# An RWKV chunk scan on 64x64 quadrants of TensorE: half of the products moved to the two quadrants left idle

## What is computed

```python
def step(S, inp):
    r_t, w_t, k_t, v_t, kk_t, b_t = inp
    sa = jnp.einsum('bhij,bhj->bhi', S, -kk_t)
    S = (S * w_t[:, :, None, :] + sa[..., None] * b_t[:, :, None, :]
         + v_t[..., None] * k_t[:, :, None, :])
    return S, jnp.einsum('bhij,bhj->bhi', S, r_t)
```

## Time and profile before

| what | value |
|---|---|
| median of 3 runs | 3131.69 us |
| the profiled execution, its own time | 3130.24 us |
| its span, first to last instruction | 3128.4 us |
| mean granted TensorE clock, share of full | 0.970 |
| busy, PE (matmul) / DVE / ACT / POOL | 93% / 57% / 34% / 41% |
| RWKV scan, loads issued to last DVE copy | 2288.0 to 2510.3 us |

### The profile page before, as it was taken

One profiled execution on the slowest core, in us unless ns is written; L12 is line 12 of the kernel. 1 busy time (PEld: TensorE's weight loads), 2 busy tenths in 40 slices (PEclk: granted clock), 3 DMA queues, 4 the chain that ended last, 5 costly groups with the idle time before them and its releaser, 6 DMA issues. The chain is left out here.

```text
span 3128.4 us, 48977 instructions
## 1 busy us (share of the span) xinstructions
PE 2918.8 (93%) x18460; PEld 2411.1 (77%) x18460; DVE 1784.2 (57%) x2599; ACT 1064.8 (34%) x1666; POOL 1283.0 (41%) x649
## 2 busy tenths in 40 slices
PE   7899889999999999999999999979869967999997
PEld 5677678887888888878888888856769855788775
DVE  1354359965777777057777777763846654333115
ACT  3366233343333333321121211244423444433223
POOL 3522333554444444444444444433344322344442
PEclk9999999999999999999999999989989998999998
DMA  3211222454444644655555555522662101222231
GB/s 120 78 58 55 75 94 78 141 147 131 165 165 164 215 169 169 208 186 197 198 189 187 193 199 195 177 80 76 206 168 54 31 14 54 71 97 94 101 101 68
DMA packets 173745, 404.23 MB, mean 129 GB/s; under 512 B 55344, under 2 KB 55472, under 8 KB 172336
## 3 DMA queue, kind: packets, MB, share of 16 engines
q1 hardware_dynamic: 173616, 402.39, 39.2%
HBM read 318.45 MB, written 83.89 MB: 129 GB/s over the span
## 5 line engine op out<-in xcount | busy, mean ns | idle before, releaser
L158 POOL TENSOR_TENSOR weights_low<-weights_raw,weights_high 128x1024 fp32r<-128x1024 f32 x435 | 1129.2, 2596 | 1597.9 <-ACT weights_high L150 1597.9
L150 ACT ACTIVATE weights_high<-weights_raw 128x1024 fp32r<-128x1024 f32 x435 | 460.7, 1059 | 1638.5 <-PE psum L258 1621.4
L256 PE MATMUL psum<-expert_in_high,weights_high 128*128 128x512 f32 x1152 | 458.3, 398 | 9.0 <-DVE expert_in_low L351 4.5
L257 PE MATMUL psum<-expert_in_low,weights_high 128*128 128x512 f32 x1152 | 449.7, 390 | 0.0
L258 PE MATMUL psum<-expert_in_high,weights_low 128*128 128x512 f32 x1152 | 449.5, 390 | 0.0
L256 PE MATMUL psum<-coefficients_high,weights_high 128*128 128x512 f32 x1024 | 399.6, 390 | 5.9 <-DVE coefficients_low L1211 4.2
L257 PE MATMUL psum<-coefficients_low,weights_high 128*128 128x512 f32 x1024 | 399.3, 390 | 0.0
L258 PE MATMUL psum<-coefficients_high,weights_low 128*128 128x512 f32 x1024 | 399.2, 390 | 0.0
L1211 DVE TENSOR_TENSOR coefficients_low<-activation_in,coefficients_high 128x512 fp32r<-128x512 f32 x128 | 354.9, 2772 | 4.4
L256 PEld LDWEIGHTS psum<-expert_in_high,weights_high 128*128 128x128 f32 x1152 | 217.1, 188 | 57.0 <-issue 9.8
L258 PEld LDWEIGHTS psum<-expert_in_high,weights_low 128*128 128x128 f32 x1152 | 216.9, 188 | 45.4
(11 more groups left out here) (381 smaller groups left out, 4647.5 us busy)
## 6 DMA issues: line engine op xcount, KB each, us to landing
weights_raw<-in_weights SPq DMA_DIRECT2D x437, 512.0 KB, 3.4
expert_activations<-expert_activation SPq DMA_DIRECT2D x128, 256.0 KB, 4.0
coefficient_table<-table_stage SPq DMA_DIRECT2D x8, 4096.0 KB, 13.1
table_group<-coefficient_table SPq DMA_DIRECT2D x128, 256.0 KB, 4.1
activation_in<-expert_activations SPq DMA_DIRECT2D x128, 256.0 KB, 3.7
chunk_b_k_v<-scan_vectors SPq DMA_DIRECT2D x8, 768.0 KB, 5.7
scan_vectors<-scan_stage SPq DMA_DIRECT2D x4, 1280.0 KB, 6.6
scan_vectors<-scan_stage SPq DMA_DIRECT2D x4, 1024.0 KB, 6.1
```

Of the source, the lines that this page charges most:

```text
L150: act.activation(d.hi[:, m % SPLIT, :], d.raw[:, m % RAW, :], ACT.Copy).then_inc(d.high, 1)
L158: pool.tensor_tensor(d.lo[:, m % SPLIT, :], d.raw[:, m % RAW, :], d.hi[:, m % SPLIT, :].bitcast(F32), ALU.subtract).then_inc(d.split, 1)
L256: pe.matmul(acc, w[0][:, cols], x[0], start=start, stop=False)
L257: pe.matmul(acc, w[0][:, cols], x[1], start=False, stop=False)
```

## The change

`product` becomes a generator with two new arguments, `side` (which half the operands lie in) and `out` (which half the result goes to). HEAD is the half in which a head's inputs lie, TOKEN the other. The scores and the turns go from HEAD to TOKEN, y goes from TOKEN to HEAD: these use the quadrants (rows 0-63, columns 64-127) and (rows 64-127, columns 0-63). Everything else stays in TOKEN, on the two quadrants that were in use. `beside` merges two products matmul pair by matmul pair.

```diff
-                def product(bank, key, g, width, terms, at=0, last=True):
+                def product(bank, key, g, width, side, out, terms, at=0, last=True):
...
-                            for r in HALVES:
-                                mm = pe.matmul(bank.ps[r, cols], lhs(r, g * H + u), rhs(r, g * H + u),
+                            for r in range(2):
+                                row = HALVES[r ^ side]
+                                mm = pe.matmul(bank.ps[HALVES[r ^ out], cols], lhs(row, g * H + u), rhs(row, g * H + u),
                                                start=(j == 0), stop=(j == len(terms) - 1))
-                    if last:
-                        mm.then_inc(bank.made, 1)
+                            if last and u == H - 1 and j == len(terms) - 1:
+                                mm.then_inc(bank.made, 1)
+                            yield
...
+                def beside(first, second, ratio=1):
+
+                    for n, _ in enumerate(first):
+                        if n % ratio == ratio - 1:
+                            next(second, None)
+                    alone(second)
...
+                    for g in range(2):
+                        if tail:
+                            alone(solve(i - 1, g))
+                        alone(grow(i, 1, g))
+                    for g in range(2):
+                        if tail:
+                            beside(itertools.chain(state(i - 1, g), times_x(i, 2, g)), y(i - 1, g))
...
+                        beside(both(grow, i, 2), scores(i + 1, 0, 0), 2)
+                        beside(both(times_x, i, 3), scores(i + 1, 0, 1), 2)
+                        beside(both(grow, i, 3), scores(i + 1, 1, 0), 2)
+                        beside(both(times_x, i, 4), scores(i + 1, 1, 1), 2)
+                        beside(both(grow, i, 4), bk_t(i + 1, 0))
+                        beside(both(times_x, i, 5), bk_t(i + 1, 1))
+                        beside(grow(i, 5, 0), v_t(i + 1, 0))
+                        beside(grow(i, 5, 1), v_t(i + 1, 1))
```

`rhs` and y leave out the term with the state for chunk 0 (it is zero), and the state after the last chunk is no longer computed. `state_out` now also waits for y of its group, since y reads the old state:

```diff
+                    if i == 0:
+                        dve.wait_ge(ends_in, 32)
+                        dve.tensor_tensor(S[:, half(g), :], view(hb[g], C), decay, ALU.mult).then_inc(hb[g].read, 1)
+                        return
+                    hb[g].taken(dve, ("S", g, i - 1))
+                    tb[g].full(dve, ("y", i))
...
-                for g in range(2):
-                    state_out(NCH - 1, g)
```

The inputs a and r are needed in both halves. They are loaded twice: with b (`front_in`), k and v (`back_in`) into two buffers `vec`, and a second time with the halves swapped (`load_ar`, two DMAs a chunk). The chunk decays are copied with swapped halves once. To make room, ar and L lie in the residual h, which is stored to DRAM in `mixer_inputs` and read back beside `gla_scan`:

```diff
                 for s in range(SLOTS):
                     w.load(sp, 0, s, SLOTS)
+                    if s == 3:
+                        sp.wait_ge(final_scaled, DC)
+                        sp.dma_start(dram["residual"], h[:, :, :]).then_inc(h_out, 16)
...
+                load_vec(0)
+                load_vec(1)
+                gla.sync(sp)
+                for r in range(2):
+                    sp.dma_start(turned_ends[HALVES[1 - r], :, :], ends[HALVES[r], :, :]).then_inc(ends_in, 16)
                 load_ar(1)
...
+                sp.dma_start(k.h[:, :, :], dram["residual"]).then_inc(h_in, 16)
+                sp.wait_ge(h_in, 16)
```

More of the change, by code:

```diff
@@ L10 @@
+import itertools
 from contextlib import ExitStack
@@ L2184, in _ @@
-                    if tail:
-                        state(i - 1, 0)
-                    times_x(i, 2, 1)
-                    if tail:
-                        y(i - 1, 1)
-                    grow(i, 2, 0)
-                    if tail:
-                        state(i - 1, 1)
-                    grow(i, 2, 1)
-                    if head:
-                        scores(i + 1, 0, 0)
-                    times_x(i, 3, 0)
-                    if head:
-                        scores(i + 1, 0, 1)
@@ L2212, in _ @@
-                    grow(i, 4, 1)
-                    if head:
-                        v_t(i + 1, 0)
-                    times_x(i, 5, 0)
-                    if head:
-                        v_t(i + 1, 1)
-                    times_x(i, 5, 1)
-                    grow(i, 5, 0)
-                    grow(i, 5, 1)
+                        alone(rhs(i - 1, 0))
+                        alone(rhs(i - 1, 1))
+                    alone(both(times_x, i, 1))
+                    for g in range(2):
+                        if tail:
+                            alone(solve(i - 1, g))
+                        alone(grow(i, 1, g))
@@ new lines, in _ @@
+                    for g in range(2):
+                        if tail:
+                            beside(itertools.chain(state(i - 1, g), times_x(i, 2, g)), y(i - 1, g))
+                        else:
+                            alone(times_x(i, 2, g))
+                    if head:
+                        beside(both(grow, i, 2), scores(i + 1, 0, 0), 2)
[6 more added lines that the diff above has]
+                        beside(grow(i, 5, 1), v_t(i + 1, 1))
+                    else:
+                        alone(both(grow, i, 2))
+                        for l in range(3, LV):
+                            alone(both(times_x, i, l))
+                            alone(both(grow, i, l))
@@ L2221, in _ @@
                 for g in range(2):
-                    rhs(NCH - 1, g)
+                    alone(rhs(NCH - 1, g))
                 for g in range(2):
-                    solve(NCH - 1, g)
+                    alone(solve(NCH - 1, g))
                 for g in range(2):
-                    y(NCH - 1, g)
-                    state(NCH - 1, g)
+                    alone(y(NCH - 1, g))
             @block.scalar
@@ L2268, in _ @@
                     gla.scalar(act, i, 1)
-                    if tail:
-                        y_out(i - 1, 0)
-                    w_out(i, 2, 0)
-                    w_out(i, 2, 1)
-                    if tail:
-                        y_out(i - 1, 1)
+                    for g in range(2):
+                        w_out(i, 2, g)
+                        if tail:
+                            y_out(i - 1, g)
                     gla.scalar(act, i, 2)
@@ L2365, in _ @@
                         k_masks(i + 1, 0)
-                    grown(i, 3, 0)
+                    for g in range(2):
+                        grown(i, 3, g)
                     if head:
                         b_masks(i + 1, 1)
-                    grown(i, 3, 1)
-                    if head:
                         k_masks(i + 1, 1)
```

162 lines of the change are left out of this document (72 added, 90 removed).

## The result

| | before | after |
|---|---|---|
| median of 7 runs each, us | 3131.27 | 3140.42 (3136.31 to 3143.03) |
| ratio, 95% interval | | 1.0029 (1.0018 to 1.0040) |
| profiled execution, its span, us | 3130.24, 3128.4 | 3140.42, 3138.4 |
| seven chunk steps, us | 175.63 | 184.47 |
| last copy of y on ACT | 2507.11 | 2515.78 |

The change is 9 us slower, a little over what a measurement can tell, and the profile agrees: the span grew by 10.0 us, the seven steps by 8.8. From the issue of the scan's first load to the last copy of y pass 226.5 us (from 2289.24) against 219.2 (from 2287.96): 7.4 of the 10.0 us lie in the scan, 1.3 ahead of it and 1.3 behind.

What follows compares the result with a forecast made beforehand. TensorE's own list of work was taken to bound the scan. Savings of 18.2 (seven steps) + 2.0 + 1.9 + 0.9 + 1.0, less 1.0, made 23 us, hence 3109 us; range 3088 to 3136.

Steps and rivals of the forecast that it cites:

- Do four quadrants run at once?: TensorE in the scan: a third and fourth quadrant likely run at once with the two in use, moving 9.1 us a step.
- The chain as the new bound: Chunk steps: with 14.0 us left on TensorE, the chain through ACT and DVE shows; 23.77 us become 20.8 to 21.4.
- The walk: Level-by-level timing of a light chunk step like 4, from its first `times_x` to the next chunk's, at 20.8 to 21.4 us.
- Rival B: TensorE in the scan: issue-bound at 29 ns a record, so four quadrants get no more; 3128 us, chance 0.12.
- Rival C: TensorE in the scan: quadrants on shared rows serialize and the order loses cover, 2.1 us a step; 3143 us, chance 0.16.
- the last state: End of the scan: 32 matmuls of 1.87 us and a DVE pair are left out, 1.9 us saved.
- the zero term: The zero state's term in rhs: 16 matmuls are left out, 0.9 us saved; in y it is hidden.
- the start: Start of the scan: the first scores wait for 768 KB instead of 1280 KB; 1.0 us saved.
- the store: The 2 MB residual store behind the mixer's fourth weight load holds the DMA engines: 1 us lost, bounds 0 and 3.
- Chunk 7: Last chunk, level 1 to level 3: 9.35 us become 7.3, 2.0 us saved.
- The second load: Second load of a and r, 0.5 MB a chunk, needed a chunk step after issue: costs nothing.
- The signs named: Changed profile: 16 `grow` matmuls beside one scores product in 0.9 to 1.0 us if right, 1.4 (B), 1.8 (C); steps 21 to 23.

Runs made afterwards that it cites:

- e3: The changed kernel with its own order but on the two quadrants of the kernel before: 3149.11 us, ratio 1.0050 to the kernel before.
- e2: The changed kernel with the order and two quadrants of the kernel before, so only storage, loads and other small parts remain: 3130.72 us, ratio 1.0000.
- e8: The kernel before plus a 512 KB DRAM to DRAM copy behind the loads of chunks 2 to 7, nobody waiting for it: 3133.44 us, ratio 1.0007.
- e10: The changed kernel with levels 4 and 5 in the order of the kernel before on TensorE and ACT: 3138.34 us, ratio 1.0021 to the kernel before.
- e11: The changed kernel with levels 1 to 3 in the order of the kernel before on all engines: 3139.49 us, ratio 1.0021 to the kernel before.
- e16: The kernel before with turns on VectorE from a swapped copy, b scores in level 3, k scores in level 4, GLA inputs loaded earlier: 3117.59 us, ratio 0.9956.
- e1b: The changed kernel plus a TensorE-only block of eight matmul series behind the scan; 512 matmuls on four quadrants: 29.1 us written out, 17.9 in a loop.

## Why the prediction was wrong

It said 3109, range 3088 to 3136, with 0.71 for faster; it is 3140, on the side that had 0.16.

- **Do four quadrants run at once?** Right, as the earlier trace rows suggested: 58 ns for four records, 17.9 us in the loop against 29.9 for two quadrants. The Trainium skill ("TensorE: Matmul & The Clock Gate", "The mechanism" of array packing) lets a weight load overlap a running matmul only when the row groups differ; read as the prediction reads it, four quadrants would have taken the 29.9 of two in the loop. The trace disagrees, and the measurement decides.
- **The chain as the new bound, 20.8 to 21.4 us a step.** This step failed. The walk let TensorE go through 14.0 us of work at 58 ns a matmul wherever its operands were ready. The steps took 23.4 to 28.9 us. For level 2 it had 2 x 1.4 us for state, `times_x` and y; they took 6.76 (2441.62 to 2448.38), with two block gaps in them (1.61 and 1.80). The sum lacked the supply of instructions: 4 for an fp32 matmul, 256 a block, 3.8 us a block; the 5.75 blocks of a step need 22 us at that pace, more than the 20.8 of the chain. A sign of it stood in the earlier trace rows, the 10.8 us of "issue" in 15 places that the prediction counted as small: 9 gaps of the kernel before, 7.9 us, stand at block bounds. The walk also had TensorE done early at each level, so that the waits of the new order looked cheap; e3 prices them at 16 to 18 us. The Trainium skill has the blocks ("Runtime: NRT & Kernel Launch", instruction fetch mechanics): 256 instructions, the next fetched while one runs, the crossing "mostly hidden". The trace agrees on the blocks and not on the price: gaps of up to 3.30 us in this kernel.
- **Rival B** asked the right question, whether 29 ns a record is the rate of feeding, and was set aside on the wrong evidence: two records that start together say nothing of the mean over a block. Its 736 x 29 (21.3 us a step; it says 21.5) is close to 5.75 blocks of 3.8. Its time, 3128, is missed too, for the order had a price of its own.
- **Rival C** had the wrong cause and nearly the right price. It put the lost cover between `grow` and the next `times_x` at 2.1 us a step, 15 in all, and tied it to quadrants that serialize. e3, the new order on the old quadrants, shows 18.4 us. Its total of 3143 is nearer to the 3140 measured than the forecast's, by luck: it has no gain by the quadrants and no block gaps. In fact the four quadrants brought, against e3, 8.7 us of the 64 (7 x 9.1) that they take off the array.
- **Small terms.** 2.8 us for the last state, the zero term, the start and the store: e2 measures 0.5, within its interval of 3 either way. The store's 1 us was not measured by itself. Chunk 7, foreseen at 7.3 us from level 1 to 3, took 10.55 (9.35 before).
- **The second load "nothing".** Not nothing for a single block: a load in the way holds it back (7.3 us where 3.8 is the pace). Spreading the loads took off 3.5 us, not certain by its interval, and adding them to the kernel before (e8) cost no time clear of the noise.
- **The signs named.** 2 x 16 `grow` records beside one scores product took 1.2 us (2448.34 to 2449.53), between the 0.9 to 1.0 of the forecast and the 1.4 of B; busy share down and waits ahead of `times_x`, as said; "wrong altogether if the steps keep 25 us" decided it.

What stays open: how much of the loss is the lower clock's, how the 18.4 us of the order fall to its parts (e10 and e11 don't add up), and how long the chain through ACT and DVE is by itself, since no run had four quadrants and instructions in time.

## What to carry to other kernels

Small fp32 matmuls written out were paid by the instruction here: count instructions per microsecond of TensorE's work before making that work faster, and look whether gaps without a releaser recur about every 128 matmul records (every 256 of all records of TensorE's stream). What covers a wait has a value of its own; measure a new order on the old hardware path first. When the supply is the limit, try moving whole operations to an engine with slack rather than running them side by side; it gave 13.9 us here (e16), though not by this alone as far as the runs tell.

## What the runs showed of the hardware

- Instructions reach TensorE in 16 KB blocks of 256. With the DMA engines idle one came every 3.5 to 4.0 us (e1b), in the scan 3.4 at the shortest (2416.46 to 2419.84), and 5.2 to 7.3 us across the loads of a chunk (768 and 512 KB). A loop of 64 instructions needed one transfer for 17.9 us.
- Four 64x64 quadrants, two of them on the same rows and two on the same columns in different PSUM banks, run matmuls and weight loads at once: 58 ns for four records, 2.09 us for 128, and 17.5 ns a record over the whole loop of e1b.
- With 16 columns the records came no faster than with 64: 262 records in 3.92 us, 15 ns a record, while the clock was still 1.00 (e1b, 2625.64 to 2629.70).
- The granted clock went to its lower level, 1.2 GHz, soon after the gap of 3.30 us in step 4, in which TensorE stood still:
```profile
2416.46:2417.60 1.14, 1.14 (x76) 1.14 (x80) 0.00 (x0) 0.00 (x0) 0.00 (x0) 1.00 0.05 14
2418.00:2421.00 3.00, 2.31 (x87) 2.13 (x84) 0.85 (x2) 0.66 (x2) 0.74 (x1) 0.50 0.01 3
```
In the series of 16 columns the clock was at 0.50 too, with TensorE busy throughout:
```profile
2652.60:2679.92 27.32, 27.32 (x1027) 27.32 (x1029) 0.00 (x0) 0.00 (x0) 0.00 (x0) 0.50 0.00 1
```
